# Routed rows listed once in DRAM, twelve raw weight slots with remainders in place, and the small rows multiplied in three groups

## The chip, the cores and the metric

The kernel runs on one core of one Trainium2 chip. The time is the device time of that core in microseconds (us), as the median of several executions; the program is launched once per execution. TensorE (PE) does the matrix products and has its own weight loads (PEld). VectorE (DVE), ScalarE (ACT) and GpSimd (POOL) do the elementwise work, SyncE (SP) issues most of the DMAs.

## The reference

One encoder block over x of 1024 rows by 1024 columns, in float32. Shortened to what matters:

```python
h = rms_norm(x, norm_mix)
x_in, b_g, c_g, q, k, v, gate_a, gate_b = split(h @ w_in)
y_conv = (b_g * conv3(c_g * x_in)) @ w_out_conv
y_attn = neighbourhood_attention(rms_norm(q), rms_norm(k), v, rpb) @ w_out_attn
x = x + (sigmoid(gate_a) * y_conv + sigmoid(gate_b) * y_attn) @ w_o
h = rms_norm(x, norm_ffn)
# 32 experts, each row goes to its top 4
logits = h @ w_router + b_router
top_v, top_i = top_k(logits, 4);  gates = softmax(top_v)
for e in range(32):                   # rows = those that chose expert e
    g = minimum(h[rows] @ w_gate[e] + b_gate[e], 7)
    u = clip(h[rows] @ w_up[e] + b_up[e], -7, 7)
    y[rows] += gate * ((g * sigmoid(1.702 * g) * (u + 1)) @ w_down[e] + b_down[e])
return x + y
```

Each expert has three weight matrices of 1024 by 1024 float32, 4 MB each.

## The kernel before, in words

The front part (projection, convolution, attention, merge, output projection, router) is the same in both kernels and fills the first 776 us or so. The change is about the expert part behind it.

**Passes.** A pass is one expert with up to 160 of its rows: 128 "large" rows, one to a partition, and up to 32 "small" rows, which the kernel keeps as four quarters of 256 columns on four groups of 32 partitions. An expert with more than 160 rows gets a second pass. A table (`table`) holds each pass's expert and a flag that says if it has small rows. The table is read into registers; the loops `Fori(0, n_loop)` on each engine run over all passes but the last two, which are written out.

**Chunks.** The weights of a pass come in 12 chunks of 1 MB: 8 for gate and up (chunk k holds rows 128k to 128k+127 of both matrices, 128 partitions by 2048), 4 for down. Pass p+1's gate and up products stand ahead of pass p's down products, so loop step p uses chunks 8 to 15 of its numbering for gate and up of pass p+1 and 16 to 19 for down of pass p (`chunk_at`). SP loads each chunk into one of 6 slots of `ring`. ACT rounds it to float32r into `w_hi` (L903), DVE writes the remainder `ring - w_hi` into `w_lo` (L1366); both have 6 slots. TensorE multiplies in three sets of four products of 512 columns: rounded rows by `w_hi` (L1853), the rows' remainder by `w_hi` (L1855), rounded rows by `w_lo` (L1869); for down these are L1904, L1906 and L1911. The semaphore `g_chunk` counts chunks that TensorE is done with; SP waits for it before it refills a slot (`room`), ACT before it refills `w_hi`.

**Small rows.** In a pass with small rows TensorE multiplies them in plain float32 by the raw chunk in `ring`, in four column groups of 32 side by side: after every second gate and up chunk (L1863, two chunks at a time) and ahead of every down chunk (L1900). One such product is two instructions in the trace. Biases are added by three-row bf16 products at the end of gate and up (L1876 small rows, L1879) and at the end of down (L1918 small rows, L1920). Each column group behind `if b > 0` is skipped where the pass has no small rows.

**Which rows a pass has.** For every pass the list of its rows is made anew. DVE takes one column of `slot_of` (L1379), GpSimd compares it with 256 slot numbers for 8 row tiles (`pick`, L660; L647 and L1479 for the first passes), TensorE multiplies `pick` by a small table of row numbers and gates, 16 products (L1823), and DVE puts row numbers and gates together (`row_numbers`, L1348 to L1360) and hands them on through `rows_new`, `rows_next`, `rows_cur` (`shift_rows`). GpSimd then gathers the rows with two indirect DMAs (L666 large, L668 small), TensorE transposes them (L1833, L1835), and the results go back with two accumulating indirect DMAs (L674, L676). GpSimd does all of this in order of its program: gather of pass p+2, scatter of pass p-1, picks of pass p+3, wait for the scatter.

The order of the work on each engine is written out by hand; nothing but semaphores ties the engines together.

## Time and profile before

| | |
|---|---|
| time, median of 3 runs (lowest to highest) | 2212.01 us (2211.32 to 2217.4) |
| time of the profiled execution | 2212.4 us |
| its span | 2210.6 us |
| mean granted TensorE clock | 0.99 |
| PE busy | 97% of the span |
| DVE busy | 70% |
| ACT busy | 51% |
| POOL busy | 39% |
| moved by DMA | 517.77 MB, mean 234 GB/s |

A busy share is over the whole span. The first 776 us are the front part, the rest the passes: the first product of pass 0 starts at 801.86 us, the last product of all at 2199.20 us. A start time in a row is counted from the span's start; where TensorE's products follow each other, the distance of two starts says what a set costs, since the durations overlap.

### The profile page before, as it was taken

The numbers are of one execution on the slowest core, as the hardware profiler recorded it, in microseconds if no ns is written. First come the engines' busy times: TensorE is split into PE (matmuls) and PEld (weight loads), VectorE is DVE, ScalarE is ACT, GpSimd is POOL, SyncE is SP. The second block draws the span as 40 slices with busy tenths as digits, with TensorE's granted clock in tenths as the row PEclk, the third lists the DMA queues.
The fourth block names the chain that finished last, engine by engine and source line by source line (L and its number), as shares of the span: only waits on it lengthen the run. The fifth ranks groups of instructions, "written<-read, shape, count | busy, mean of one in ns | idle before, by whom it ended". The sixth has DMA issues, their size and how long they took to land.

```text
span 2210.6 us, 36392 instructions
## 1 busy us (share of the span) xinstructions
PE 2149.8 (97%) x11540; PEld 1538.5 (70%) x11541; DVE 1545.9 (70%) x1940; ACT 1129.8 (51%) x1138; POOL 867.7 (39%) x486
## 2 busy tenths in 40 slices
PE   8999999999999969999999999999999999999997
PEld 6874554787888847776666767676776666677775
DVE  5544333535335589998777877788788787788896
ACT  4433223424222146676555656575666565575674
POOL 1343121000000046767444645454555464454751
PEclk9999999999999979999999999999999999999999
DMA  6421110333334278999888888898898898898996
GB/s 232 94 81 53 39 47 10 86 86 105 88 103 153 106 278 307 377 368 329 295 285 286 310 303 304 299 338 298 299 355 318 280 313 305 282 322 298 354 360 221
DMA packets 206010, 517.77 MB, mean 234 GB/s; under 512 B 19168, under 2 KB 86624, under 8 KB 205952
## 3 DMA queue, kind: packets, MB, share of 16 engines
q1 hardware_dynamic: 190016, 470.97, 58.5%
q0 software_dynamic: 15936, 46.02, 9.7%
q8 instruction: 37, 0.61, 0.1%
q14 instruction: 21, 0.17, 0.0%
HBM read 480.68 MB, written 32.05 MB: 232 GB/s over the span
## 4 chain that ended last, share of the span: by engine, by line
PE 81%; issue 5%; DMA 4%; POOL 4%; DVE 3%; ACT 1%; SPq 1%; DVEq 0%; POOLq 0%; ACTq 0%
PE psum L1869 9%; PE psum L1853 9%; PE psum L1855 8%; PE psum L1649 7%; PE psum L1904 5%; PE psum L1863 5%; PE psum L1906 5%; PE psum L1911 4%; PE psum L1670 4%; PE psum L1669 4%; PE psum L1671 4%; PE psum L1900 3%; POOL rs L610 2%; DMA ring<-in_w_up 2%; POOL pick L660 1%
## 5 line engine op out<-in xcount | busy, mean ns | idle before, releaser
L1366 DVE TENSOR_TENSOR w_lo<-ring,w_hi 128x2048 fp32r<-128x2048 f32 x383 | 871.5, 2300 | 98.9 <-ACT w_hi L903 88.5
L903 ACT ACTIVATE w_hi<-ring 128x2048 fp32r<-128x2048 f32 x384 | 728.4, 1920 | 364.7 <-DMA ring<-in_w_up 237.5
L660 POOL TENSOR_SCALAR pick<-iota_bf,slot_col 128x256 bf16<-128x256 bf16 x244 | 475.5, 1963 | 143.9 <-DVE slot_col L1379 143.9
L1869 PE MATMUL psum<-w_lo,xT_hi 128*128 128x512 f32 x992 | 276.0, 400 | 1.9 <-DVE w_lo L1366 1.9
L1853 PE MATMUL psum<-w_hi,xT_hi 128*128 128x512 f32 x992 | 274.0, 398 | 1.6 <-DVE gt L1386 1.4
L1855 PE MATMUL psum<-w_hi,xT_lo 128*128 128x512 f32 x992 | 267.0, 391 | 0.0
L1869 PEld LDWEIGHTS psum<-w_lo,xT_hi 128*128 128x128 f32 x992 | 180.5, 188 | 92.6 <-issue 31.0
L666 POOL DMA_INDIRECT xg<-h_rows,idx_new x32 | 68.1, 2128 | 433.8 <-DVE idx_new L1360 421.2
L1855 PEld LDWEIGHTS psum<-w_hi,xT_lo 128*128 128x128 f32 x992 | 186.8, 188 | 40.7
L1853 PEld LDWEIGHTS psum<-w_hi,xT_hi 128*128 128x128 f32 x992 | 181.5, 188 | 44.7 <-issue 8.3
L1649 PE MATMUL psum<-hT,ring 128*128 128x512 f32 x384 | 174.2, 601 | 0.0
L634 POOL TENSOR_TENSOR rstd<-var,half 128x1 f32<-128x1 f32 x8 | 4.4, 555 | 409.5 <-DVE var L1308 409.5
L1904 PE MATMUL psum<-w_hi,aT_hi 128*128 128x512 f32 x496 | 146.7, 418 | 0.1
L1906 PE MATMUL psum<-w_hi,aT_lo 128*128 128x512 f32 x496 | 134.3, 393 | 0.0
L1911 PE MATMUL psum<-w_lo,aT_hi 128*128 128x512 f32 x496 | 133.2, 390 | 0.0
L1649 PEld LDWEIGHTS psum<-hT,ring 128*128 128x128 f32 x384 | 70.0, 190 | 81.2 <-issue 81.2
L1184 DVE TENSOR_TENSOR ring_lo<-ring,gate_hi 128x2048 fp32r<-128x2048 f32 x16 | 36.7, 2291 | 121.8 <-ACT gate_hi L813 121.8
L1863 PE MATMUL psum<-ring,xTb 128*32 128x512 f32 x960 | 115.4, 598 | 0.0
L1904 PEld LDWEIGHTS psum<-w_hi,aT_hi 128*128 128x128 f32 x496 | 85.3, 189 | 41.0 <-issue 28.3
L1906 PEld LDWEIGHTS psum<-w_hi,aT_lo 128*128 128x128 f32 x496 | 93.7, 189 | 21.5
L1911 PEld LDWEIGHTS psum<-w_lo,aT_hi 128*128 128x128 f32 x496 | 93.2, 188 | 20.3
L628 POOL TENSOR_TENSOR bias<-masks,win 128x384 f32<-128x384 bf16 x48 | 44.0, 938 | 154.0 <-DVE nmin L1109 137.4
(350 smaller groups left out, 3301.9 us busy)
## 6 DMA issues: line engine op xcount, KB each, us to landing
ring<-in_w_gate SPq DMA_DIRECT2D x256, 512.0 KB, 5.4
ring<-in_w_up SPq DMA_DIRECT2D x256, 512.0 KB, 6.6
ring<-in_w_down SPq DMA_DIRECT2D x256, 512.0 KB, 6.3
ring<-in_w_in SPq DMA_DIRECT2D x44, 512.0 KB, 5.2
ring<-in_x SPq DMA_DIRECT2D x16, 512.0 KB, 3.8
ring<-in_w_in SPq DMA_DIRECT2D x6, 1024.0 KB, 6.5
vb<-oT SPq DMA_DIRECT2D x16, 256.0 KB, 6.7
ring<-in_w_oc SPq DMA_DIRECT2D x16, 256.0 KB, 3.0
```

The source lines that it names most:

```text
L660: e.tensor_scalar(pick[:, t, :], iota_bf[:, :], slot_col[:, t, :], None, ALU.is_equal).then_inc(g_pick, 1)
L903: e.activation(w_hi[:, hs, :], ring[:, slot, :], ACT.Copy).then_inc(g_hi, 1)
L1366: e.tensor_tensor(w_lo[:, hs, :], ring[:, slot, :], w_hi[:, hs, :].bitcast(F32), ALU.subtract).then_inc(g_lo, 1)
L1649: ins = e.matmul(bank[m % 2][:, :], wv[:, k, :], hT[:, k, 512 * hf:512 * hf + 512], start=(k == 0), stop=(k == KT - 1))
L1669: e.matmul(dst, w_up, up, start=start, stop=False)
L1853: e.matmul(bank[i][:, :], hi[:, k, :], w_hi[:, hs, 512 * i:512 * i + 512], start=(k == 0), stop=False)
L1855: e.matmul(bank[i][:, :], lo[:, k, :], w_hi[:, hs, 512 * i:512 * i + 512], start=False, stop=False)
L1863: e.matmul(bank[6][QT * j:QT * j + QT, :].rearrange("p (g n) -> p g n", g=2), small[:, kb % 2, QT * (kb // 2):QT * (kb // 2) + QT], pair[: ...
L1869: ins = e.matmul(bank[i][:, :], hi[:, k, :], w_lo[:, hs, 512 * i:512 * i + 512], start=False, stop=False)
L1904: e.matmul(bank[4 + h][:, :], aT_hi[:, k, :], w_hi[:, hs, at0:at0 + 512], start=(k == 0), stop=False)
L1906: e.matmul(bank[4 + h][:, :], aT_lo[:, k, :], w_hi[:, hs, at0:at0 + 512], start=False, stop=False)
L1911: ins = e.matmul(bank[4 + h][:, :], aT_hi[:, k, :], w_lo[:, hs, at0:at0 + 512], start=False, stop=False)
```

## The change

It has four parts.

1. **Lists of all passes at once.** DVE works out for each of the 4096 choices (row, expert) its place in a list of all passes (`full_turns`, `list_places`, `places_of_choices`, `entry_places`), GpSimd writes row number and gate there with 32 indirect DMAs of 128 entries of 8 bytes (`put_entries`) into a DRAM tensor `lists`, and reads the whole of it back with five DMAs (`lists_back`). From pass 3 on GpSimd copies a pass's column out of it (`gather`, `current`). Passes 0 to 2 still take their rows from `pick` products. The picks, the 16 products, `row_numbers` and `shift_rows` leave the loop. The gates of pass 0 are made on their own (`gates_of_first`).
2. **Twelve raw slots.** Instead of 6 raw slots and 6 of `w_lo` there are 12 raw slots (`ring` and `late_raw`), and the remainder is written over the raw chunk it is made from (`raw_of`, `lo_of`). Chunk 0 of pass 0 alone puts its remainder into slot 11. A slot is refilled when the chunk 12 back is done. SP's loop order changes with it: it now starts with chunk 12 of a step.
3. **Small rows in three groups.** Gate and up of a pass with small rows are two groups of four chunks: the first in the last down chunk of the step before, the second in chunk k=2; down is one group, in chunk k=6. A group waits until its four chunks have landed. As the remainder would overwrite what the group reads, DVE waits (`small_taken`) for TensorE's first product behind the group before it goes on.
4. **Biases elsewhere.** The gate and up bias comes behind the transposes of chunk 3, the down bias behind down chunk 2; the last product of the last chunk now ends the sums and signals them.

The diff, cut:

```diff
-NSLOT = 6
+RING = 6
+NSLOT = PASS_CHUNKS
...
+        def raw_of(c0):
+            slot = c0 % NSLOT
+            return ring[:, slot, :] if slot < RING else late_raw[:, slot - RING, :]
+        def lo_of(c0):
+            slot = NSLOT - 1 if c0 == 0 else c0 % NSLOT
+            return ring_lo[:, slot, :] if slot < RING else late_lo[:, slot - RING, :]
...
             def room(p, c0):
-                c = c0 - NSLOT
-                hold(e, g_chunk, 12 * p + (c + 1 + (c in PAIRED)))
+                hold(e, g_chunk, 12 * p + (c0 - NSLOT + 1))
...
             def loads_of_pass(p, last):
-                for k in range(GU_CHUNKS):
+                for k in range(4, GU_CHUNKS):
                     room(p, 8 + k)
                     load_gate_up(p, 8 + k, k, exn)
...
+                    exnn = e.value_load(table[0:1, bass.ds(p + 2, 1)], min_val=0, max_val=E - 1)
+                    for k in range(4):
+                        room(p, 20 + k)
+                        load_gate_up(p, 20 + k, k, exnn)
...  (GpSimd)
+            def gather(n):
+                hold(e, g_xtr, n)
+                e.tensor_copy(idx_new[:, :], idx_all[:, bass.ds(n, 1), :]...).then_inc(l_new, 1)
+                hold(e, l_new, n - 2)
+                gather_rows()
+            def current(n):
+                e.tensor_copy(idx_cur[:, :], idx_all[:, bass.ds(n, 1), :]...).then_inc(l_cur, 1)
+                e.tensor_copy(gate_cur[:, :], lists_in[:, :, bass.ds(n, 1), 1]...).then_inc(l_cur, 1)
+                hold(e, l_cur, 2 * n)
+                e.sem_inc(g_free, 1)
+            def put_entries(js):
+                for j in js:
+                    e.indirect_dma_start(out=lists, out_offset=bass.IndirectOffsetOnAxis(ap=dest[:, j:j + 1], axis=0),
+                                         in_=entry[:, j, :], in_offset=None).then_inc(l_put, 16)
+            def lists_back():
+                hold(e, l_put, 16 * TT * TOPK)
+                e.dma_start(lists_in[:, 0, :, :]..., lists_a).then_inc(l_back, 16)
+                for j in range(4):
+                    e.dma_start(lists_in[QT * j:QT * j + QT, 1, :, :]..., lists_b).then_inc(l_back, 16)
+                hold(e, g_col, 2)
+                hold(e, l_back, 80)
...
-            gather(0, True)
-            gather(1, False)
-            pick_tokens(2, 4)
+            first_gather(0)
+            hold(e, g_copy, 1)
+            e.sem_inc(g_free, 1)
+            hold(e, l_dest, 1)
+            hold(e, list_fill, 32)
+            put_entries(range(3))
+            first_gather(1)
+            put_entries(range(3, 12))
+            first_gather(2)
+            put_entries(range(12, TT * TOPK))
+            lists_back()
             with e.Fori(0, n_loop) as p:
-                gather(p + 2, False)
                 with e.If(p > 0):
+                    gather(p + 2)
                     scatter(p)
-                pick_tokens(p + 3)
-                with e.If(p > 0):
                     scattered(p)
-                e.sem_inc(g_free, 1)
+                    current(p)
...  (VectorE)
+            def small_taken(b, groups):
+                with e.If(b > 0):
+                    hold(e, g_small, groups)
...
                 swiglu(p, hb)
+                small_taken(hbn, 3 * p + 4)
                 rest_of_weights(p, 8 + 4)
-                slots_of(p + 3, exn)
...
+                small_taken(hb, 3 * p + 5)
                 for c in range(2):
                     rest_of_weights(p, 16 + c)
...
                 rest_of_rows(p + 2, xT_hi, xT_lo, 0)
-                shift_rows(p, False)
-                row_numbers(p + 3, 6)
+                small_taken(hb2, 3 * p + 6)
                 rest_of_weights(p, 12 + 8)
...  (TensorE)
+            def small_gate_up(p, c0, ks, b, rows, small=xTb, evacuated=None, ends=False):
+                with e.If(b > 0):
...
+                    landed_chunks(p, range(c0, c0 + len(ks)))
+                    hold(e, g_xhi, rows)
+                    for i, k in enumerate(ks):
+                        pair = raw_of(c0 + i).rearrange("p (g n) -> p g n", g=2)
+                        for j in range(4):
+                            e.matmul(bank[6][QT * j:QT * j + QT, :]..., small[:, k % 2, ...],
+                                     pair[:, :, QD * j:QD * j + QD], start=(k == 0), stop=(ends and k == KT - 1))
...
+                def second_rows():
+                    small_gate_up(p, 12, range(4, KT), hbn, 2 * p + 3)
+                def down_rows():
+                    small_down(p, 16, hb, 2 * p + 1, bank[7])
+                def next_rows():
+                    small_gate_up(p, 20, range(4), hb2, 2 * p + 5)
+                for k in range(1, GU_CHUNKS):
+                    gate_up(p, 8 + k, k, aside={2: second_rows, 6: down_rows}.get(k), signals_small=k in (2, 6))
+                    if k == 3:
+                        act_transpose(p, hb, 4, 7)
+                        gate_up_bias(p + 1, hbn)
                 e.wait_ge(g_alo, 2 * p + 2)
                 for c in range(D_CHUNKS):
-                    down(p, 16 + c, c, hb, aside=third_expert if c == 1 else None)
+                    down(p, 16 + c, c, aside=next_rows if c == 3 else None, signals_small=c == 3)
                     if c == 1:
                         rows_transpose(p + 2, 0, 2)
                     if c == 2:
-                        slot_rows(p + 3, flags["ex3"], 6)
-                down_bias(p, hb)
+                        down_bias(p, hb)
```

**GpSimd behind the first gather.** `xg` and `xgb` are the gathered large and small rows, `out_rows` the result. Before, from the gather of pass 1 into the loop:

```order
L666 DMA xg<-h_rows,idx_new 128x1024
L668 DMA xgb<-h_rows,idx_new 128x256
L660 TENSOR_SCALAR pick<-iota_bf,slot_col 128x256 x4
L687 TENSOR_LOAD table
L687 ISA x2
L688 UNCONDITIONAL_BRANCH
L688 ISA
L415 REGISTER_ALU
L666 DMA xg<-h_rows,idx_new 128x1024
L668 DMA xgb<-h_rows,idx_new 128x256
L690 COMPARE_AND_BRANCH
L415 ISA
```

Now, from behind the gather of pass 0 to the loop:

```order
L717 DMA lists<-entry,dest 10240x2 x3
L691 DMA xg<-h_rows,idx_new 128x1024
L693 DMA xgb<-h_rows,idx_new 128x256
L717 DMA lists<-entry,dest 10240x2 x9
L691 DMA xg<-h_rows,idx_new 128x1024
L693 DMA xgb<-h_rows,idx_new 128x256
L717 DMA lists<-entry,dest 10240x2 x20
L722 DMA lists_in<-lists 128x128
L724 DMA lists_in<-lists 32x128 x4
L727 CAST slot_of<-lists_in 128x64
L728 TENSOR_SCALAR slot_of<-lists_in,quarter 128x64
```

The puts (L717) stand ahead of and between the gathers of passes 1 and 2, and all 32 of them, the reading back (L722, L724) and two copies stand ahead of the loop, whose first gather is that of pass 3.

**TensorE, end of gate and up in the loop.** Here `xTb` and `aTb` are the small rows and their activations. Before, from the small rows of the last two chunks to those of the first down chunk:

```order
L1859 COMPARE_AND_BRANCH
L1863 MATMUL psum<-ring,xTb 32x512 x8
L1859 UNCONDITIONAL_BRANCH
L1869 MATMUL psum<-w_lo,xT_hi 128x512 x4
L415 ISA
L1874 COMPARE_AND_BRANCH
L1876 MATMUL psum<-brow_gu,ones_bf 32x512 x4
L1874 UNCONDITIONAL_BRANCH
L1879 MATMUL psum<-brow_gu,ones_bf 128x512 x4
L1895 REGISTER_ALU
L1896 COMPARE_AND_BRANCH
L1900 MATMUL psum<-ring,aTb 32x256 x8
```

Now, from chunk 6 to the start of down:

```order
L1973 MATMUL psum<-w_hi,xT_lo 128x512 x4
L1955 COMPARE_AND_BRANCH
L1938 ISA
L1961 MATMUL psum<-ring,aTb 32x256 x16
L1961 MATMUL psum<-late_raw,aTb 32x256 x16
L1955 UNCONDITIONAL_BRANCH
L1980 MATMUL psum<-ring_lo,xT_hi 128x512 x4
L1967 REGISTER_ALU
L1971 MATMUL psum<-w_hi,xT_hi 128x512 x4
L1973 MATMUL psum<-w_hi,xT_lo 128x512 x4
L1980 MATMUL psum<-ring_lo,xT_hi 128x512 x4
L2008 REGISTER_ALU
```

The bias and the small products between gate and up and down are gone from this seam; the small products of all four down chunks stand in chunk 6 in one group, and DVE's remainder of down chunk 0 waits for the product behind them.

**TensorE, end of a loop step.** `pick` by `rows_bf` are the products of the list of pass p+3. Before:

```order
L1823 MATMUL psum<-rows_bf,pick 128x6 x9
L1895 REGISTER_ALU
L1896 COMPARE_AND_BRANCH
L1900 MATMUL psum<-ring,aTb 32x256 x8
L1896 UNCONDITIONAL_BRANCH
L1904 MATMUL psum<-w_hi,aT_hi 128x512 x4
L1906 MATMUL psum<-w_hi,aT_lo 128x512 x4
L1911 MATMUL psum<-w_lo,aT_hi 128x512 x4
L415 ISA
L1916 COMPARE_AND_BRANCH
L1918 MATMUL psum<-brow_d,ones_bf 32x256 x4
L1916 UNCONDITIONAL_BRANCH
```

Now:

```order
L2028 COMPARE_AND_BRANCH
L2030 MATMUL psum<-brow_d,ones_bf 32x256 x4
L2028 UNCONDITIONAL_BRANCH
L2032 MATMUL psum<-brow_d,ones_bf 128x512 x2
L2008 REGISTER_ALU
L2011 MATMUL psum<-w_hi,aT_hi 128x512 x4
L2013 MATMUL psum<-w_hi,aT_lo 128x512 x4
L1942 COMPARE_AND_BRANCH
L1938 ISA
L438 REGISTER_ALU
L1950 MATMUL psum<-late_raw,xTb 32x512 x16
L1942 UNCONDITIONAL_BRANCH
```

The list products and the small products of each down chunk are gone, the bias stands ahead of the last down chunk, and in this chunk stand the small products of the next pass's first four chunks.

## Rows read from the trace of the kernel before

**Rows 1.** The page: busy time, share of the span, instructions.

```profile
PE 2149.8 (97%) x11540; PEld 1538.5 (70%) x11541; DVE 1545.9 (70%) x1940; ACT 1129.8 (51%) x1138; POOL 867.7 (39%) x486
```

**Rows 2.** Windows: us; PE, PEld, DVE, ACT, POOL busy (count); PEclk, DMA share, GB/s.

```profile
860.00:1014.00 154.00, 149.71 (x738) 118.00 (x737) 141.36 (x140) 107.48 (x84) 105.11 (x49) 0.99 0.99 360
...
829.00:2199.00 1370.00, 1355.11 (x7805) 968.45 (x7805) 1142.81 (x1152) 854.45 (x698) 737.09 (x363) 1.00 0.90 315
```

**Rows 3.** TensorE's timeline (start, us), plain passes: waits in brackets.

```profile
867.14 1.35 PE L1823 MATMUL psum<-rows_bf,pick 128*128 x16 [1.18 <-POOL pick L660]
...
902.12 1.04 PE L1833 MATMUL psum<-ident,xg 128*128 128x128 f32 x8
...
939.99 1.09 PE L1833 MATMUL psum<-ident,xg 128*128 128x128 f32 x8 [0.56 <-DVE ut L1388]
```

**Rows 4.** TensorE's timeline, gate and up of a pass with small rows.

```profile
1311.02 1.07 PE L1853 MATMUL psum<-w_hi,xT_hi 128*128 128x512 f32 x4
1311.92 1.07 PE L1855 MATMUL psum<-w_hi,xT_lo 128*128 128x512 f32 x4
1312.92 1.92 PE L1863 MATMUL psum<-ring,xTb 128*32 128x512 f32 x16
1314.77 1.21 PE L1869 MATMUL psum<-w_lo,xT_hi 128*128 128x512 f32 x4
1315.82 1.09 PE L1853 MATMUL psum<-w_hi,xT_hi 128*128 128x512 f32 x4
```

**Rows 5.** TensorE's timeline, down of a pass with small rows.

```profile
1343.30 1.07 PE L1911 MATMUL psum<-w_lo,aT_hi 128*128 128x512 f32 x4
1344.29 1.07 PE L1900 MATMUL psum<-ring,aTb 128*32 128x256 f32 x16
1345.29 1.21 PE L1904 MATMUL psum<-w_hi,aT_hi 128*128 128x512 f32 x4
1346.34 1.09 PE L1906 MATMUL psum<-w_hi,aT_lo 128*128 128x512 f32 x4
```

**Rows 6.** TensorE's timeline, a list made between two down chunks.

```profile
1304.46 0.56 PE L1823 MATMUL psum<-rows_bf,pick 128*128 x16
1304.87 1.17 PE L1904 MATMUL psum<-w_hi,aT_hi 128*128 128x512 f32 x4
1305.88 1.08 PE L1906 MATMUL psum<-w_hi,aT_lo 128*128 128x512 f32 x4
```

**Rows 7.** Groups by line and shape: count, busy us, mean ns, idle before.

```profile
L1863 PE MATMUL psum<-ring,xTb 128*32 128x512 f32 x960 | 115.4, 598 | 0.0
L1900 PE MATMUL psum<-ring,aTb 128*32 128x256 f32 x960 | 64.2, 385 | 0.0
...
L1823 PE MATMUL psum<-rows_bf,pick 128*128 x512 | 19.3, 166 | 2.3 <-POOL pick L660 2.3
...
L1876 PE MATMUL psum<-brow_gu,ones_bf 3*32 3x512 bf16 x60 | 5.9, 385 | 0.0
```

**Rows 8.** GpSimd's timeline: a start instruction, then the gathers of passes 1 and 2.

```profile
7.33 0.58 POOL L600 TENSOR_TENSOR rstd<-var,half 128x1 f32<-128x1 f32 x1
...
809.61 2.33 POOL L666 DMA_INDIRECT xg<-h_rows,idx_new  x1 [15.11 <-DVE idx_new L1360]
812.25 1.90 POOL L668 DMA_INDIRECT xgb<-h_rows,idx_new  x1 [0.31 <-issue]
...
832.94 1.01 POOL L666 DMA_INDIRECT xg<-h_rows,idx_new  x1 [5.79 <-DVE idx_new L1360]
834.26 3.08 POOL L668 DMA_INDIRECT xgb<-h_rows,idx_new  x1 [0.31 <-issue]
```

**Rows 9.** VectorE's timeline: the picks of pass 1, and remainders in pass 1.

```profile
802.93 1.66 DVE L1479 TENSOR_SCALAR pick<-iota_bf,slot_col 128x256 bf16<-128x256 bf16 x8
...
834.21 6.69 DVE L1366 TENSOR_TENSOR w_lo<-ring,w_hi 128x2048 fp32r<-128x2048 f32 x3 [2.25 <-ACT w_hi L903]
```

**Rows 10.** Instructions that touch the gathered rows: time from issue to landing.

```profile
DMA to landing us min/median/max: 4.6/7.0/9.5
```

More of the change, by code:

```diff
@@ L531, in _ @@
             e.wait_ge(g_gatb, 16)
-            for k in range(MSLOT, NSLOT):
+            for k in range(MSLOT, GU_CHUNKS):
                 load_gate_up(0, k, k, 0)
@@ L653, in _, with gather_rows @@
             e.wait_ge(x1_out[1], 16 * TT // 2)
-            def pick_tokens(n, many=TT):
-                hold(e, g_col, n)
-                hold(e, g_imm, n)
-                for t in range(many):
-                    e.tensor_scalar(pick[:, t, :], iota_bf[:, :], slot_col[:, t, :], None, ALU.is_equal).then_inc(g_pick, 1)
-            def gather(n, first):
-                hold(e, g_rows, n + 1)
-                if not first:
-                    hold(e, g_xtr, n)
+            def gather_rows():
                 e.indirect_dma_start(out=xg[:, :], out_offset=None, in_=h2_rows,
@@ L1463, in _ @@
             gates_of(TT - 2)
+            gates_of_first()
+            full_turns(5, 7)
             e.wait_ge(f_row, 2)
@@ L1857, in gate_up @@
                     aside()
-                if extra:
-                    with e.If(b > 0):
-                        for kb in extra:
-                            pair = ring[:, (c0 + kb - k) % NSLOT, :].rearrange("p (g n) -> p g n", g=2)
-                            for j in range(4):
-                                e.matmul(bank[6][QT * j:QT * j + QT, :].rearrange("p (g n) -> p g n", g=2), small[:, kb % 2, QT * (kb // 2):QT * (kb // 2) + QT],
-                                         pair[:, :, QD * j:QD * j + QD], start=(kb == 0), stop=False)
                 if hi is aT_hi and k == 0:
@@ L1891, in act_transpose, with down @@
                 ins.then_inc(g_atr, 1)
[L1893 removed]
+            def down(p, c0, c, aside=None, signals_small=False):
                 at, slot, hs, _ = chunk_at(p, c0)
                 e.wait_ge(g_hi, at + 1)
[L1896 to L1901 removed]
                 halves = [(k, h, D * (k % 2) + 512 * h) for k in (2 * c, 2 * c + 1) for h in range(2)]
@@ L1909, in down @@
                 e.wait_ge(g_lo, at + 1)
-                for k, h, at0 in halves:
-                    ins = e.matmul(bank[4 + h][:, :], aT_hi[:, k, :], w_lo[:, hs, at0:at0 + 512], start=False, stop=False)
+                for n, (k, h, at0) in enumerate(sorted(halves, key=lambda part: part[1])):
+                    last = k == KT - 1
+                    ins = e.matmul(bank[4 + h][:, :], aT_hi[:, k, :], lo_of(c0)[:, at0:at0 + 512], start=False, stop=last)
+                    if signals_small and n == 0:
+                        ins.then_inc(g_small, 1)
+                    if last and h == 0:
+                        ins.then_inc(g_d, 1)
                 ins.then_inc(g_chunk, 1)
@@ L2008, in part @@
                     for k in (2 * c, 2 * c + 1):
-                        off = D * (k % 2)
-                        if small:
-                            with e.If(b > 0):
-                                for j in range(4):
-                                    e.matmul(bank[2][QT * j:QT * j + QT, 0:QD], xTb[:, k % 2, QT * (k // 2):QT * (k // 2) + QT],
-                                             ring[:, slot, off + QD * j:off + QD * j + QD], start=(k == 0), stop=False)
-                        at0 = off + 512 * h
@@ L2016, in part @@
-                        product(bank[3 + 3 * h][:, :], xT_hi[:, k, :], xT_lo[:, k, :], w_hi[:, hs, at0:at0 + 512], w_lo[:, hs, at0:at0 + 512], k == 0, False)
-                def bias(h, small):
-                    if small:
-                        with e.If(b > 0):
-                            for j in range(4):
-                                e.matmul(bank[2][QT * j:QT * j + QT, 0:QD], ones_bf[0:3, 0:QT], brow_d[0:3, QD * j:QD * j + QD], start=False, stop=True)
+                        at0 = D * (k % 2) + 512 * h
@@ L2028, in last_down @@
-                part(3, 0, True)
+                    part(c, 0)
+                    part(c, 1)
+                part(2, 0)
+                part(3, 0)
                 hold(e, g_bd, 32 * n_loop + 64)
-                bias(0, True)
-                part(2, 1, False)
-                part(3, 1, False)
-                bias(1, False)
+                with e.If(hbe > 0):
+                    for j in range(4):
+                        e.matmul(bank[2][QT * j:QT * j + QT, 0:QD], ones_bf[0:3, 0:QT], brow_d[0:3, QD * j:QD * j + QD], start=False, stop=True)
@@ L2034, in _ @@
+                bias(0)
+                part(2, 1)
+                part(3, 1)
+                bias(1)
             e.wait_ge(g_ev, 2 * n_loop + 1)
             e.wait_ge(g_xlo, 2 * n_loop + 4)
[L2036 to L2042 removed]
```

400 lines of the change are left out of this document (223 added, 177 removed).

## The prediction

> **What bounds the kernel now.** I read the busy shares first: PE 97%, DVE 70%, POOL 39% [rows 1]. TensorE is nearly never idle, so what counts is the work in its queue and who stops it. Then the windows: over the passes TensorE is idle for 1370.0 - 1355.1 = 14.9 us in all, and DMA is busy 0.90 of the time [rows 2]. The window of the plain passes (no small rows) differs: DMA share 0.99 at 360 GB/s. It has 738 products, and a plain pass has 184 (144 of weights, 18 transposes, 16 for the list, 6 for biases), so these are four passes of 38.5 us. So plain passes run at the memory's pace and the others at TensorE's. Then TensorE's timeline, for the distances of starts: a set of four products costs 0.90 us (1311.02 to 1311.92) [rows 4], and in the plain passes one sees short waits, 1.18 us for GpSimd's picks and 0.56 us for VectorE [rows 3]. Last the groups by line, for counts [rows 7]: L1876 has 60 instructions, four a pass, so 15 of the 32 passes have small rows; L1823 has 512, sixteen a list, so 32 lists.
>
> **Small rows in three groups.** L1855 to L1869 with a group between takes 1314.77 - 1311.92 = 2.85 us, the set itself 0.90, and the set behind it 1.05 for 0.90: the group costs 2.10 us [rows 4]. Its 16 instructions go four at a time; three rounds take (1.92 - 0.60) / 3 = 0.44 each (0.598 is one instruction [rows 7]), so four rounds are 1.76 and changing over and back 0.34. For down: 1345.29 - 1343.30 - 0.90 + 0.15 = 1.24 us, rounds of (1.07 - 0.385) / 3 = 0.23, four are 0.92, the rest 0.32 [rows 5, 7]. All products stay, only changes go: 4 groups become 2 for gate and up, 4 become 1 for down, five changes of 0.33 a pass. 15 x 5 x 0.33 = 25 us less, all of it on the path since TensorE has no idle time in these passes. Bounds: 15 us (if rounds of different chunks do not join well) to 30.
>
> **Lists off TensorE.** A list costs 1304.87 - 1304.46 = 0.41 us and 0.11 on the set behind it (1.01 for 0.90) [rows 6]: 0.52. Passes 3 to 31 lose theirs, 29 x 0.52 = 15 us less. VectorE's list work (some 2.5 us a pass in small steps) and GpSimd's picks go too; both lie beside TensorE's products and are worth nothing by themselves.
>
> **Biases.** Same products in other seams. In a pass with small rows the gate bias used to share its change-over with the first down group and now does not: 15 x 0.2 = 3 us more, from the 0.33 above; between 0 and 5.
>
> **Twelve slots.** A plain pass needs 38.5 us of DMA but, without its waits and the list, about 36 of TensorE. Small rows add 4 x 2.10 + 4 x 1.24 = 13.4 to that, and such a pass has DMA time to spare. With 12 chunks of room the lead gained in such passes, or while TensorE waits, carries over plain ones. What it can give is the idle time that is left, 14.9 us [rows 2], less the start, the tail and what VectorE's own order makes: I take 7, between 2 and 12.
>
> **New holds of VectorE.** 15 passes have three places where VectorE may not write the remainder before TensorE's first product behind the group. From there TensorE has the rest of the set (0.7) and two sets of the next chunk (1.8 and 0.15 for the change) before it needs the remainder in the worst place (the group in the last down chunk): 2.65 us. VectorE needs 2.23 (6.69 / 3) [rows 9] and a semaphore or two. I take 2 us over all passes; 0 at the low end, the high end is a rival below. At the other two places a whole chunk more lies between. The groups also wait for four landed chunks; with the ring full that is covered, and at the first pass with small rows, behind a run of plain ones, it is just covered by my count.
>
> **The lists on GpSimd.** This is the dear new part. The 32 puts start when VectorE has the places: its picks end at 804.6 [rows 9], two new operations over 1024 elements are 1.1 each by the 2.23 for 2048 elements [rows 9], with small ones and what shifts earlier about 808.5. The trace has no put; the nearest rows are gathers of the same 128 entries. Alone one takes 1.01 us; while VectorE works on remainders 1.90, 2.33 and 3.08 [rows 8]. The 3.08 is telling: it starts at 834.26, VectorE's remainders run from 834.21 in steps of 2.23 [rows 9], and it ends 0.9 us after the first of them. So such a DMA waits for the end of the operation that runs, then gets through, one in each 2.23 us at worst when they follow each other. With 0.3 us of issue: 1.3 to 3.4 a put. I take 2.1, since VectorE is at this work most but not all of the time. 32 x 2.1 = 67, the gathers of passes 1 and 2 between them 2 x 4.8 = 10: the last put ends at 885. Landing 3 more, five DMAs back at 1.9 each, the shorter gather's row (897), their landing 4.6 [rows 10], copies and branches 2: 903. Then the gather of pass 3: two issues (2.5) and 7 to the landing of the second [rows 10]: 912. TensorE transposed these rows at 902.12 before [rows 3] and would now be there about 899 (the picks' wait gone, the start and VectorE's first pass 2 us later). It waits 13 us and comes 10 us later than before, plus 1 for the slower clock behind an idle stretch. Ends: at 1.3 a put nothing waits, at 3.4 the wait grows by 42.
>
> The Trainium skill (SBUF — State Buffer, section "Who interferes with whom") speaks against my price: a VectorE operation with two SBUF inputs, as the remainder is, takes only the read side of the shared port pair, and making descriptors is inferred not to be held up by it. By that rule each put would take about the time it takes alone, and the rival without a list wait below would come true. The trace does not agree so far: 1.01 alone against 3.08 beside the remainder [rows 8].
>
> The GpSimd instruction at 7.33 starts without a wait, straight behind the fills ahead of it [rows 8]; five more small ones stand there now and make all that follows some 1 us later. That is inside the 808.5 above.
>
> **Sum**, against the profiled execution's 2212.4 (span 2210.6, 1.8 us around it that stay): list wait +10 + 1, the start inside it, biases +3, holds +2, small groups -25, lists -15, slots -7: -31, so 2181.4. The median of the runs shown is 0.4 below the profiled execution: 2181.
>
> **The rivals.**
> No list wait: puts at 1.3 us end near 860 and the first gather out of the list is issued about 887, ahead of 899. TensorE is then 3 us early where I have it 10 late, and the clock stays: 2181 - 14 = 2167. For it: 1.01 for a gather while VectorE idles. Against it: the other three gathers took 1.90 to 3.08 [rows 8].
> Dear puts (the slower side): each put at 3.4, as the 3.08 row plus issue. 32 x 1.3 more = 42: 2223. It decides from 3.07 a put, where 31 us are eaten. For it: one row; against it: back to back they should meet a boundary every 2.23.
> Late remainders: each of the 45 holds costs one remainder, 2.23: 100 us more, 2281. It makes the kernel slower from 0.7 a hold. Against it: 2.65 us of cover at the tightest place.
> Memory keeps its pace: the 4096 small writes and the deeper loads share the DMA engines, the slots give nothing and the groups wait for landed chunks at each return from plain passes, seven or eight times 2 us: 2181 + 7 + 8 = 2196. For it: the share of 0.99 [rows 2].
>
> **Chances and range.** Forecast 0.54, no list wait 0.26, memory 0.06, dear puts 0.05, late remainders 0.04; 0.05 for mixtures that end level. What a measurement of this kernel can tell from no change is about 0.3%, 6.6 us. Faster 0.86, same 0.05, slower 0.09. The forecast's own range is 2170 to 2195; to hold 8 in 10 it reaches to the case without a list wait and most of the memory case: 2160 to 2204.
>
> **What would show it.** TensorE waits once for `xg` or `xgb` near 900 to 912, and GpSimd's 32 puts fill 808 to 885; no such wait means the second case. A group of 32 small gate products takes about 3.9 us with its changes, a down group 4.0. L1823's successor has 32 instructions. In plain passes the evacuations are 36 us apart, not 38.5. I am wrong if TensorE shows idle time for remainders in each pass with small rows, or if puts are over 3 us each.

## The result, and the profile after

The changed kernel takes 2188.6 us (median of 4, 2187.1 to 2190.6), the kernel before 2213.7 us on the same chip (2211.3 to 2217.4). The ratio is 0.9887, 95% interval 0.9873 to 0.9901: 25.1 us less, where 31 were forecast (2181). The profiled execution took 2189.2 us, its span is 2187.5.

The page's busy shares of after, against [rows 1]. GpSimd goes from 39% to 22%:

```profile
PE 2128.6 (97%) x11060; PEld 1540.4 (70%) x11061; DVE 1482.0 (68%) x1474; ACT 1114.2 (51%) x1138; POOL 482.8 (22%) x377
```

The windows of after, the plain passes and all passes, against [rows 2] (length; busy us and instructions of each engine; clock, DMA share, GB/s):

```profile
860.00:1014.00 154.00, 146.35 (x665) 116.36 (x664) 134.43 (x81) 105.55 (x84) 62.77 (x47) 0.98 0.99 358
829.00:2176.00 1347.00, 1335.10 (x7350) 972.74 (x7349) 1083.60 (x696) 841.94 (x702) 349.66 (x247) 1.00 0.90 318
```

TensorE now idles 11.9 us over the passes, where it was 14.9. What is behind them stands in its waits (engine, line, releaser: us in total, times, longest):

```profile
PE psum L1924 <- DMA xgb<-h_rows,idx_new: 7.7, 1, 7.7
PE psum L1931 <- DVE late_lo L1447: 1.6, 1, 1.6
PE psum L1971 <- DVE gt L1472: 0.9, 1, 0.9
PE psum L2003 <- DVE ut L1484: 0.7, 1, 0.7
PE psum L1980 <- issue: 0.7, 1, 0.7
PE psum L1971 <- DVE ut L1474: 0.2, 1, 0.2
```

One wait of 7.7 us is the forecast list wait. Without it 4.2 us are left where there were 14.9; the waits for POOL's picks [rows 3] are gone with the rest. Behind the list wait the granted clock is 0.50 from 909 to 913 us, the lower of its two levels (1.2 GHz), and 0.92 from 913 to 917; it was 1.00 from 860 to 901.

GpSimd's timeline shows how the list wait comes about (start, us, engine, line, operation, idle before it):

```profile
833.68 0.97 POOL L717 DMA_INDIRECT lists<-entry,dest  x1 [0.31 <-issue]
...
847.33 1.90 POOL L717 DMA_INDIRECT lists<-entry,dest  x1 [0.30 <-issue]
849.53 1.90 POOL L717 DMA_INDIRECT lists<-entry,dest  x1 [0.30 <-issue]
...
882.43 1.89 POOL L717 DMA_INDIRECT lists<-entry,dest  x1 [0.30 <-issue]
889.77 0.60 POOL L722 DMA_DIRECT2D lists_in<-lists  x1 [5.44 <-DMA lists<-entry,dest]
890.37 2.05 POOL L724 DMA_DIRECT2D lists_in<-lists  x4
897.01 0.24 POOL L727 CAST slot_of<-lists_in 128x64 uint32<-128x64 f32 x1 [4.60 <-DMA lists_in<-lists]
...
901.27 2.30 POOL L691 DMA_INDIRECT xg<-h_rows,idx_new  x1 [0.83 <-POOL idx_new L704]
903.87 0.98 POOL L693 DMA_INDIRECT xgb<-h_rows,idx_new  x1 [0.30 <-issue]
```

All 32 puts in one line of their source's view (min/median/max in ns, first and last start in us), and the start of TensorE's transposes for pass 3, which was at 902.12 before [rows 3]:

```profile
L717 POOL DMA_INDIRECT lists<-entry,dest x32: 968/1894/3089, 809.5 to 882.4; - x32
```
```profile
909.17 1.96 PE L1924 MATMUL psum<-ident,xg 128*128 128x128 f32 x8 [7.65 <-DMA xgb<-h_rows,idx_new]
```

A pass with small rows, TensorE's timeline, against [rows 4, 5]:

```profile
1315.38 1.10 PE L1973 MATMUL psum<-w_hi,xT_lo 128*128 128x512 f32 x4
1316.41 3.64 PE L1950 MATMUL psum<-ring,xTb 128*32 128x512 f32 x32
1319.98 1.19 PE L1980 MATMUL psum<-late_lo,xT_hi 128*128 128x512 f32 x4
1321.01 1.09 PE L1971 MATMUL psum<-w_hi,xT_hi 128*128 128x512 f32 x4
1321.94 1.09 PE L1973 MATMUL psum<-w_hi,xT_lo 128*128 128x512 f32 x4
```
```profile
1332.24 1.09 PE L1973 MATMUL psum<-w_hi,xT_lo 128*128 128x512 f32 x4
1333.26 1.93 PE L1961 MATMUL psum<-ring,aTb 128*32 128x256 f32 x32
1335.01 1.91 PE L1961 MATMUL psum<-late_raw,aTb 128*32 128x256 f32 x32
1336.85 1.20 PE L1980 MATMUL psum<-ring_lo,xT_hi 128*128 128x512 f32 x4
1337.88 1.09 PE L1971 MATMUL psum<-w_hi,xT_hi 128*128 128x512 f32 x4
```

A group costs 1319.98 - 1316.41 and 0.10 on either side, 3.8 us; down is the same. That is as forecast (3.9 and 4.0). But look at the sets: 1321.01 to 1321.94 is 0.93 us for four products, where it was 0.90 [rows 4]. It is so nearly everywhere. Over the pairs of weight products that follow each other directly (less than 300 ns from start to start, 4092 pairs before and 4268 after), the mean distance of starts is 232.7 ns in after and 228.9 ns before. There are 4608 such products in either kernel, so this is 17.5 us that no term of the forecast had. The experiments begin with it.

### The profile page after: what moved, and what is told of

Read it like the earlier page. It is cut to its first block, busy times and chain, and to the rows that moved or that the text cites. A ratio compares the mean times of both kernels' runs of the same rounds, so it can differ in the third digit from the quotient of the medians.

```text
span 2187.5 us, 34658 instructions
## 1 busy us (share of the span) xinstructions
PE 2128.6 (97%) x11060; PEld 1540.4 (70%) x11061; DVE 1482.0 (68%) x1474; ACT 1114.2 (51%) x1138; POOL 482.8 (22%) x377
## 4 chain that ended last, share of the span: by engine, by line
PE 86%; POOL 5%; issue 4%; DVE 2%; DMA 2%; ACT 0%; SPq 0%; POOLq 0%; DVEq 0%; ACTq 0%
PE psum L1980 10%; PE psum L1971 10%; PE psum L1973 10%; PE psum L1738 7%; PE psum L2011 5%; PE psum L2019 5%; PE psum L2013 5%; PE psum L1950 5%; PE psum L1758 4%; PE psum L1760 4%; PE psum L1759 4%; POOL lists L717 3%; PE psum L1961 2%; POOL rs L645 2%; PE psum L1851 1%
## 5 line engine op out<-in xcount | busy, mean ns | idle before, releaser
L1447 DVE TENSOR_TENSOR late_lo<-late_raw,w_hi 128x2048 fp32r<-128x2048 f32 x192 | 432.9, 2288 | 116.9 <-PE psum L2019 100.6
L1447 DVE TENSOR_TENSOR ring_lo<-ring,w_hi 128x2048 fp32r<-128x2048 f32 x191 | 427.2, 2284 | 92.7 <-PE psum L1980 92.0
L969 ACT ACTIVATE w_hi<-late_raw 128x2048 fp32r<-128x2048 f32 x192 | 363.7, 1921 | 1.2 <-PE psum L1980 0.8
L969 ACT ACTIVATE w_hi<-ring 128x2048 fp32r<-128x2048 f32 x192 | 354.3, 1924 | 12.3 <-DMA ring<-in_w_up 12.3
L704 POOL COPY idx_new<-slot_of 128x2 uint32 x29 | 28.6, 987 | 507.7 <-PE psum L1926 504.9
L1980 PE MATMUL psum<-late_lo,xT_hi 128*128 128x512 f32 x496 | 139.0, 402 | 0.8 <-issue 0.7
L1980 PE MATMUL psum<-ring_lo,xT_hi 128*128 128x512 f32 x496 | 136.1, 396 | 0.0
L1980 PEld LDWEIGHTS psum<-late_lo,xT_hi 128*128 128x128 f32 x496 | 90.7, 188 | 40.1 <-issue 13.7
L734 POOL DMA_INDIRECT out_rows<-ys,idx_cur x31 | 65.4, 2109 | 207.3 <-ACT ys L998 206.6
L1980 PEld LDWEIGHTS psum<-ring_lo,xT_hi 128*128 128x128 f32 x496 | 92.0, 188 | 26.9 <-issue 6.2
```

The source lines that it names most:

```text
L969: e.activation(w_hi[:, hs, :], raw_of(c0), ACT.Copy).then_inc(g_hi, 1)
L1447: e.tensor_tensor(lo_of(c0), raw_of(c0), w_hi[:, hs, :].bitcast(F32), ALU.subtract).then_inc(g_lo, 1)
L1980: ins = e.matmul(bank[i][:, :], hi[:, k, :], lo_of(c0)[:, 512 * i:512 * i + 512], start=False, stop=(k == KT - 1))
```

## The experiments

Each was timed beside the kernel before on its chip. "Distance" is the mean over the pairs just named; for one kind of product it is taken from its start to the next one's. The moving operand is the weights (`w_hi`, `late_lo`, `ring_lo`), the stationary one the rows or activations (`xT`, `aT`). An address is a byte within a partition.

**e1 and e2, where the weights lie.** The change replaces three small tensors ahead of w_hi by one, and w_hi and everything behind it slide down by 32 bytes. e1 is the changed kernel, e2 the kernel before, each with the place of the other:

```diff
-        sb("w_pad", [P, 152], where=moe)
+        sb("w_pad", [P, 160], where=moe)    # e1; e2 has 144
```

> The changed kernel with the unused tensor w_pad ahead of w_hi 8 floats longer: w_hi begins at byte 130976 of a partition instead of 130944 and late_raw/late_lo at 180128 instead of 180096, that is 32 bytes behind a multiple of 64 as in the kernel before (and as the ring, which neither kernel moves). Nothing else differs. Theory A (place): the fp32r products of 512 columns stand 232.7 ns apart in the changed kernel and 228.9 ns in the one before because of where their moving operand lies; then the distance goes back to about 229 ns, and 4608 products x 3.8 ns = 17.5 us go: 2171 us. Rival B (traffic): the products are slower because weights are changed in place or because VectorE and the queues write at other times; then the distance stays 232.7 ns and the time 2188.6 +- 2 us.

Measured: 2168.4 us (ratio 0.9795, 0.9767 to 0.9822), distance 227.8 ns.

> The kernel before with w_pad 8 floats shorter: w_hi at byte 130944 and w_lo at 180096, multiples of 64 as in the changed kernel. Theory A (place): the products of 512 columns go from 228.9 to about 232.7 ns apart and the time from 2213.7 to 2231 us. Rival B (traffic): no change, 2213.7 +- 2 us.

Measured: 2226.5 us (ratio 1.0063, 1.0042 to 1.0084), distance 233.1 ns. The same products of TensorE in the same window (count: ns min/median/max, first and last start), before and after, then e1, then e2:

```profile
L1853 PE MATMUL psum<-w_hi,xT_hi x32: 389/389/504, 986.0 to 1007.9; 128*128 128x512 f32 x32
```
```profile
L1971 PE MATMUL psum<-w_hi,xT_hi x35: 392/396/503, 970.7 to 1007.7; 128*128 128x512 f32 x35
```
```profile
L1971 PE MATMUL psum<-w_hi,xT_hi x36: 389/389/499, 971.4 to 1007.9; 128*128 128x512 f32 x36
```
```profile
L1853 PE MATMUL psum<-w_hi,xT_hi x32: 392/396/502, 985.3 to 1007.3; 128*128 128x512 f32 x32
```

The place is the cause: it goes with 32 bytes of address in both kernels and in both directions, while e1 has the same in-place remainders and the same transfers as the changed kernel. e1 gives back 20 us; its distance alone would give 4608 x 4.9 = 22.6, but its list wait is longer (9.0 us for 7.7). e2 costs 14, not the 4608 x 4.2 = 19 of the distance: in the kernel before 5 us of slower products were covered. Three plain passes show some of it (from one evacuation to the next): they take 38.3, 38.1 and 38.3 us in e2 and 38.5, 38.4 and 37.9 before, with the memory 0.99 busy in both, so they kept the memory's pace and did not feel the products. By 144 products of 4.2 ns a pass that is some 2 us of the 5 (an estimate); where the rest was covered is open. In the changed kernel the two plain passes behind the list wait take 36.5 us each, in e1 36.2 and 35.8.

**e8, e10, e11 and e12, what of the place counts.** The distance depends on the stationary operands (aT, xT) too. e8 moves them with the rest:

```diff
+        sb("x_pad", [P, 8], where=moe)
         xg = sb("xg", [P, D], where=moe)
```

and w_pad is 152 (e8), 144 (e10), 160 (e12); e11 has w_pad 176 and no x_pad.

> The changed kernel with 8 unused floats ahead of xg: w_hi and late_raw lie at 130976 and 180128 as in e1, but the stationary operands (aT, xT and the rest of the small tensors) also lie 32 bytes higher, at a multiple of 64. Theory A1: the place of the moving operand alone sets the distance; 227.8 ns and 2168 us as in e1. Rival A2: what counts is that the stationary and the moving operand lie alike by 64; in e1 both are 32 off a multiple of 64, here and in the changed kernel they differ; then 232.7 ns and 2188 us.

Measured: 2191.4 us, distance 233.1 ns. With w_hi at the very address of e1, all is slow again: A1 falls.

> e8 with w_pad 16 floats shorter: the stationary operands of the products (aT, xT) and the moving operands in w_hi and late_lo all begin at multiples of 64, only the six slots of the ring (and so ring_lo, a sixth of the products) stay 32 bytes off one. Theory A2 (alike): moving and stationary alike by 64 give 228 ns; the products of w_hi and late_lo return to 228 to 229 ns, those of ring_lo stay near 233 ns, and the time is 2188.6 - 15 = 2173 us. Rival A3 (both off): only 32 bytes off on both sides is fast; all products stay at 233 ns, 2191 us.

Measured: 2190.0 us; w_hi with xT_hi 232.6 ns, with xT_lo 233.4, late_lo 233.5. Both at multiples of 64, and slow: theory A2, alike by 64, falls as I had put it.

> The changed kernel with w_pad 176 floats: w_hi at byte 131040 and late_raw at 180192, 96 bytes behind a multiple of 128 where the stationary operands and the ring stand 32 behind one. Theory: alike by 64 is what counts; 228 ns and 2168 us as in e1. Rival: it goes by 128 (or more); then the products of w_hi and late_lo stay near 233 ns and the time near 2188 us.

Measured: 2179.4 us, distance 230.0 ns, between the two values expected: a placement alike by 64 is not enough here either.

> e8 with w_pad 8 floats longer: the stationary operands at 64 behind a multiple of 128 and the moving ones in w_hi and late_lo too, so that they lie alike by 512 as in e1 (there both 32 behind a multiple of 128), but at a multiple of 64; the ring stays 32 behind. So far: alike, both 32 off: 227.8 ns (e1); moving 96 against 32: 230.0; 0 against 32: 232.7; 32 against 64: 233.1; 0 against 64: 232.4 to 233.5. Theory A4 (alike by 128): the products of w_hi and late_lo come to 228 to 229 ns, and the time to about 2173 us. Rival A3 (neither on a multiple of 64): all stay at 232.5 to 233.5 ns, 2190 us.

Measured: 2176.3 us; w_hi with xT_lo 227.6 ns, late_lo 227.9, w_hi with xT_hi (which comes behind the ring's products) 229.6, ring_lo 233.8. TensorE's timeline of e12 has both kinds one behind the other: the set of L1974 (w_hi, alike) is 0.91 us long to the next start, that of L1981 (ring_lo, not alike) 0.94. The set of L1972, alike too, takes 0.93:

```profile
972.71 1.07 PE L1974 MATMUL psum<-w_hi,xT_lo 128*128 128x512 f32 x4
973.62 1.10 PE L1981 MATMUL psum<-ring_lo,xT_hi 128*128 128x512 f32 x4
974.56 1.09 PE L1972 MATMUL psum<-w_hi,xT_hi 128*128 128x512 f32 x4
975.49 0.85 PE L1974 MATMUL psum<-w_hi,xT_lo 128*128 128x512 f32 x3
```

So the relative place of the two operands counts. The fastest products begin alike by 128 bytes: 32 and 32 (e1), 64 and 64 (w_hi with xT_lo and late_lo in e12). A difference of 32 costs 5 ns a product, one of 64 between 2 and 5. But alike is not enough by itself. `ring_lo` and xT_hi are at the same two places, both 32 behind a multiple of 128, in the changed kernel, in e1 and in e11, and their products are 230.7, 227.3 and 230.5 ns apart: these are slowed where only w_hi and late_lo were moved. What carries over from the other products no run shows. Which power of two above 64 counts was not taken further: the fast pairs of e1 and e12 are alike even by 512. Nor is it explained why the kernel before, whose operands are alike as in e1, stood at 228.9 ns and not at 227.8.

**e3, the list wait.** The last 8 puts are left out, so the lists lack a quarter of their entries; the work per pass stays:

```diff
-                hold(e, l_put, 16 * TT * TOPK)
+                hold(e, l_put, 16 * 24)
...
-            put_entries(range(12, TT * TOPK))
+            put_entries(range(12, 24))
```

> The changed kernel with the last 8 of the 32 puts of list entries left out (a quarter of the tokens' entries is missing from the lists of passes 3 and on; all passes do the same work on other rows). Theory: the puts cost 2.1 us each, so the lists are back 16 us earlier, TensorE's wait of 7.8 us for the rows of pass 3 goes and the slow clock of 2 us behind it with it: 10 us less, about 2179 us, with the rows' transposes in the place that the kernel before had them. Rival: the weights are what TensorE would wait for there (the memory is busy 0.99 in that stretch); then a wait for weights takes the place of most of the 7.8 us and the time stays above 2185 us.

Measured: 2178.6 us (ratio 0.9842, 0.9816 to 0.9869), 10.0 us under the changed kernel. TensorE has no wait over 0.9 us up to 1100 us, and pass 2 takes 36.5 us instead of 46.5. All other passes keep their length. The list wait costs 10 us, and no other wait stood behind it: the rival, weights that come late, is out.

**e4, the groups.** Each group is cut in two, at the two seams of its chunk (the helpers' change and the same step in `down` are left out here):

```diff
-                def second_rows():
-                    small_gate_up(p, 12, range(4, KT), hbn, 2 * p + 3)
+                second_rows = halved(lambda i: small_gate_up(p, 12, range(4, KT), hbn, 2 * p + 3, part=i))
...                                   # down_rows and next_rows likewise
                 for i in range(4):
                     e.matmul(bank[i][:, :], hi[:, k, :], w_hi[:, hs, 512 * i:512 * i + 512], start=(k == 0), stop=False)
+                if isinstance(aside, tuple):
+                    aside[0]()
+                    aside = aside[1]
```

> The changed kernel with each of the three groups of small-row products in a pass cut in two, one half between the first and second set of its chunk and one between the second and third: 45 more groups over the 15 passes with small rows, the same products. Theory (the forecast's term): 75 groups fewer gave 25 us, 0.33 us each, so 45 more cost 15 us: about 2203 us. Rival, from the distances between products in the two traces: a group costs 0.14 us of its own, so 45 more cost 6 us: about 2195 us, and then less than half of the forecast's 25 us came from the merging.

Measured: 2202.9 us (ratio 0.9956, 0.9944 to 0.9968), 14.3 us more, 0.32 us for each of the 45 groups. The rival, 0.14 us a group, is out.

**e6, the list products.** On e1:

```diff
                     if k == 3:
+                        e.wait_ge(g_pick, 3 * TT)
+                        hold(e, g_y, 2 * p + 2)
+                        for b in range(2):
+                            for t in range(TT):
+                                e.matmul(bank[7][:, 400 + 3 * b:403 + 3 * b], pick[:, t, P * b:P * b + P], rows_bf[:, t, 0, :], start=(t == 0), stop=(t == TT - 1))
                         act_transpose(p, hb, 4, 7)
```

> e1, with 16 list products of 128x3 per pass put back on TensorE in each of the 30 passes of the loop, ahead of the transposes of the activations; their sums go into unused columns and are read by nobody. Theory (the forecast's term for lists off TensorE, 15 us): 0.5 us a pass, about 2183 us. Rival: they cost their whole 0.6 us of busy time and the change to and from the fp32r products besides, 0.8 us a pass or more: 2192 us. Other rival: they fall into time in which TensorE would wait for the activations anyway; then 2168 us.

Measured: 2181.2 us (ratio 0.9861, 0.9845 to 0.9878), 12.9 us over e1, 0.43 us for each of 30 lists (13.5 and 0.45 over e7 below, which was on the same chip and is as fast as e1). That is less than their busy time in the groups by line, 16.6 us, which overlaps that of the products on either side:

```profile
L2091 PE MATMUL psum<-rows_bf,pick 128*128 128x3 bf16 x480 | 16.6, 165 | 0.0
```

**e7, fewer slots ahead.** On e1:

```diff
-                hold(e, g_chunk, 12 * p + (c0 - NSLOT + 1))
+                hold(e, g_chunk, 12 * p + (c0 - 9 + 1))
```

> e1, with the load of each chunk from the twelfth on let go when the chunk nine before it is through, not twelve. Theory: nothing waits for weights with twelve slots, and the transfers have spare time behind 950 us (the memory is busy 0.90 there), so nine give the same within 2 us: 2168 us. Rival: the groups of small rows need four chunks at once, one of them only six ahead of its load then; TensorE waits in each of the 15 passes with small rows, 1 us or more each: 2183 us or more.

Measured: 2167.7 us (ratio 0.9796, 0.9779 to 0.9812), as e1. Nine chunks ahead are as good as twelve. Whether six would do with merged groups was not run, so how much of the gain needs more than six slots is not shown.

**e5 and e9, a version without the list wait.** e5 is e1 with pass 3 listed by picks as passes 1 and 2 are:

```diff
...                                   # addresses as in e1; holds and registers left out
-            put_entries(range(12, TT * TOPK))
+            put_entries(range(12, 26))
+            first_gather(3)
+            e.sem_inc(l_new, 1)
+            put_entries(range(26, TT * TOPK))
...                                   # POOL's loop
-                with e.If(p > 0):
+                with e.If(p > 1):
                     gather(p + 2)
+                with e.If(p > 0):
                     scatter(p)
...                                   # VectorE's loop, at its head
+                with e.If(p < 1):
+                    slots_of(3, ex3)
+                    first_picks(3, range(TT))
...                                   # and behind rest_of_act
+                with e.If(p < 1):
+                    row_numbers(3, 7, col=400)
...                                   # TensorE's loop, behind chunk 1
+                        with e.If(p < 1):
+                            slot_rows(3, ex3, 7, col=400).then_inc(g_imm, 1)
```

> e1 (w_hi at byte 130976), with the list of pass 3 made as those of passes 1 and 2 are, by picks on VectorE and 16 products on TensorE in pass 0, so that its rows are fetched amid the puts (behind the 26th) and the lists are wanted one pass later. Theory: TensorE's wait for the rows of pass 3 (9.0 us in e1, with about 2 us of slow clock behind it) goes; the picks and products cost 2 to 3 us on TensorE's path at most: e1's 2168.4 less 8 to 11, 2159 us. Rival: the wait only moves, to the rows of pass 4 or to weights or remainders that come late behind the picks on VectorE; then the time stays above 2165 us.

Measured: 2173.0 us (ratio 0.9821, 0.9804 to 0.9837), 5 us more than e1. The wait had moved. TensorE's row in the timeline of e5, and ScalarE's behind it:

```profile
924.03 2.07 PE L1984 MATMUL psum<-w_hi,xT_hi 128*128 128x512 f32 x4 [6.88 <-ACT w_hi L973]
```
```profile
920.92 0.69 ACT L998 ACTIVATE ys<-psum,gate_cur 128x512 f32<-128x512 f32 x1 [11.09 <-POOLq L713]
921.50 0.68 ACT L1002 ACTIVATE ys<-psum,gate_cur 128x512 f32<-128x512 f32 x1
922.08 1.91 ACT L973 ACTIVATE w_hi<-late_raw 128x2048 fp32r<-128x2048 f32 x1
```

ScalarE stands at the outputs, which want the gates of pass 1, and the rounding of the next weights is queued behind. L713 is GpSimd's signal that these gates are in place. GpSimd's own rows in e5 say what held it:

```profile
904.08 0.32 POOL L728 TENSOR_SCALAR slot_of<-lists_in,quarter 128x64 uint32<-128x64 f32 x1
907.33 2.71 POOL L734 DMA_INDIRECT out_rows<-ys,idx_cur  x1 [2.92 <-issue]
910.34 2.57 POOL L736 DMA_INDIRECT out_rows<-ysb,idx_cur  x1 [0.30 <-issue]
920.45 0.18 POOL L710 COPY idx_cur<-slot_of 128x2 uint32 x1 [7.54 <-DMA out_rows<-ysb,idx_cur]
920.58 0.17 POOL L711 COPY gate_cur<-lists_in 128x2 f32 x1
```

The lists are there at 904.4, and the gates are copied out of them only at 920.6. Between stands the first scatter, which GpSimd issues behind the reading back and whose landing it waits for. In e1 this was hidden beside TensorE's own list wait (the gates come at 913.6 there). e9 issues the first scatter ahead of the reading back:

```diff
             put_entries(range(26, TT * TOPK))
+            scatter(1)
             lists_back()
...                                   # POOL's loop
                 with e.If(p > 1):
                     gather(p + 2)
-                with e.If(p > 0):
                     scatter(p)
+                with e.If(p > 0):
                     scattered(p)
```

> e5 with the first scatter of outputs issued right behind the last put, ahead of the reading back of the lists, instead of behind it. In e5 TensorE waits 6.9 us at 924 us for a rounding that stands on ScalarE behind the outputs of pass 1, and these for the gates of pass 1 out of the lists and for the first scatter. Theory: the list is wanted in two places, by the rows of pass 3 and by those gates; with both relieved nothing waits there and e5's 2173.0 loses 7 to 10 us: 2164 us, faster than e1 (2168.4). Rival: the memory, busy 0.99 to 1.03 in these stretches, then holds weights back; TensorE waits for them instead and the time stays at 2171 us or more.

Measured: 2163.5 us (ratio 0.9778, 0.9754 to 0.9801). The lists are there at 903.5, about as in e5, and the gates at 907.8: the scatter was the wait. It is the fastest of all, 48 us under the kernel before on its chip and 25 under the changed one, and leaves out nothing. Its runs (2162.4 to 2164.6) meet neither those of e1 (2165.9 to 2169.5), which were on another chip, nor those of e7 on its own (2166.4 to 2168.9). Its waits up to 1100 us hold no list:

```profile
PE psum L1994 <- DVE late_lo L1455: 1.6, 1, 1.6
PE psum L1985 <- DVE gt L1480: 0.9, 1, 0.9
PE psum L1994 <- issue: 0.7, 1, 0.7
PE psum L1985 <- DVE ut L1482: 0.2, 1, 0.2
```

## Why the prediction was right, and where a term was missing

| term | forecast | measured | from |
|---|---|---|---|
| list wait and slow clock behind it | +11 | +10.0 | e3 |
| small groups, 75 fewer | -25 | -23.9 | e4, 0.32 x 75 |
| lists off TensorE | -15 | -12.9 | e6, 0.43 x 30 |
| other idle time | -7 | -10.7 | windows and waits, 14.9 to 4.2 |
| biases and holds | +5 | not apart | |
| distance of the products | 0 | +17.5 | 4608 x 3.8 ns; e1, e2 |

The measured terms sum to -20.0, and the change is -25.1. The 5 us between them no term has, and they are more than 5 by whatever biases and holds cost. e2 found 5 us of slower products that did not show in the kernel before; that these are the same was not tested.

The first row compares unlike things. The forecast's +11 counts from the kernel before; against a kernel without a list wait it had 14 (its rival at 2167). e3 measures the latter, so in like terms the wait came out 4 us too dear.

**The puts.** Forecast: from 808.5 to 885 us, 2.1 us each with issue. They run from 809.5 to 884.3 with a median of 1.89 and 0.3 of issue. What I argued from a single row [rows 8] holds: nine puts take 0.97 to 0.99 us, as at 833.68, where VectorE works out of PSUM. The 23 others take 1.08 to 3.09, and each of them ends 0.84 to 0.88 us behind the end of a VectorE operation with both inputs in SBUF. So such a put waits for the end of the operation that runs and then gets through, one for each remainder when these follow each other. The put at 847.33 ends at 849.23, and the first of these three remainders (2.28 us each) at 848.38:

```profile
846.10 6.69 DVE L1447 TENSOR_TENSOR ring_lo<-ring,w_hi 128x2048 fp32r<-128x2048 f32 x3
```

The Trainium skill (SBUF — State Buffer, section "Who interferes with whom") infers that the making of descriptors is not held up by a VectorE operation with two SBUF inputs; here it is, by 0.1 to 2.1 us a put. The rival without a list wait, 2167, wanted puts of 1.3 us with issue and falls.

**The rows of pass 3.** Forecast 912 for their landing and 10 us later than before; they come at about 909 and TensorE starts 7 us later (909.17 for 902.12). The step that was too dear is the reading back. I gave each of its five DMAs the 1.9 us of a put; they take 0.6 and 0.5 (L722, L724), 7 us less in all. Part of this was lost again: the last put lands 5.4 us after its end where I took 3, and from the landing of the lists to the first gather it is 4.3 us where I took 2. (My steps to 903 also add up to 904.) TensorE is ready for the rows at 901.5, not at 899, so it waits 7.7 us and not 13. The clock took more in return: e3 gives 10.0 for 7.7 of idle time, where I had 1 for the clock.

**Groups and lists** came within 1.1 and 2.1 us. I had counted 29 lists where 30 go (32 lists before [rows 7], 32 products, that is 2, now), and the price of one was 0.43 us, not 0.52. Both were read from distances of starts on either side of a seam, not from busy times.

**Twelve slots.** 10.7 us of idle time went where I took 7, but the reason is only half shown. Plain passes no longer keep the memory's pace (36.5 us for 38.5, 36 forecast) while the memory is as busy as before (0.99 from 860 to 1014). That fits chunks that were loaded ahead; yet e7 does it with nine.

**The step that failed** is "all products stay". They did, each 3.8 ns dearer, because 32 bytes of small tensors had gone in front of w_hi. It is the second largest term. That the time lies only 7.6 us above the forecast is in part luck: against the 17.5 stand 3.7 us of idle time beyond what I took, and 10 us that are no merit of the working: the 5 forecast for biases and holds, which nothing here shows, and the 5 that no term has. The other rivals (memory keeps pace, dear puts, late remainders) left hardly a trace: no wait for weights, no put over 3.1 us, one late remainder of 1.6 us (L1931), at the tail. The price of the memory rival was also added up wrongly: seven or eight waits of 2 us are 15, not 8, and make 2203, not 2196.

## What to carry to other kernels

Where TensorE is 97% busy, a change that moves no product can still move their operands: compare addresses, and the distance of starts of one plain kind of product, before counting anything else. Price a seam from the starts on both sides of it. When a wait is taken away, look at what else is queued on the engine that caused it: here the rows of pass 3 came earlier, but the gates of pass 1 still stood behind the reading back and a scatter in GpSimd's order, and took over most of the wait.

## What the runs showed of the hardware

- The distance of back-to-back 128x512 fp32r products depends on where their operands lie in a partition. Where all moving and stationary operands begin alike by 128 bytes it is 227.8 ns in e1 and 228.9 in the kernel before; with the moving ones 32 bytes off, or the stationary ones, it is 232.7 to 233.1 (after, e2, e8). In a kernel with both kinds, products that are themselves alike can be slowed too: 230.7 ns for ring_lo with xT_hi in after, 227.3 in e1. The Trainium skill (SBUF — State Buffer, section "Who interferes with whom") gives TensorE two independent read ports for the two; the runs show that their addresses are not independent of each other.
- An indirect DMA of 128 entries of 8 bytes takes GpSimd 0.97 us where VectorE idles or works out of PSUM. Beside VectorE operations with both inputs in SBUF it takes up to 3.09 and ends 0.84 to 0.88 us behind the end of one of them (23 puts of after). GpSimd's plain DMAs took 0.5 to 0.6 us each while a remainder ran (VectorE's three remainders below cover L722 and L724 above):

```profile
889.00 6.68 DVE L1447 TENSOR_TENSOR ring_lo<-ring,w_hi 128x2048 fp32r<-128x2048 f32 x3
```
